# The final norm of a hybrid decoder: two of four token tiles finished by GpSimd and ScalarE instead of VectorE

## What is computed

```python
def rmsnorm(x, w):
    xf = x.astype(jnp.float32)
    y = xf * lax.rsqrt(jnp.mean(xf * xf, axis=-1, keepdims=True) + NORM_EPS)
    return (y * w.astype(jnp.float32)).astype(x.dtype)

def reference(x, ...):
    ...
        h = h + hier_moe(hn, router_group_w[l], router_group_b[l], router_expert_w[l],
                         router_expert_b[l], expert_w_gate[l], expert_w_up[l], expert_w_down[l])
    return rmsnorm(h, final_norm_w)
```

## Time and profile before

| | us |
|---|---|
| median of 3 runs | 2718.67 |
| the three runs | 2718.04, 2718.67, 2720.47 |
| the profiled execution's own time | 2721.2 |
| its span, first to last instruction | 2719.5 |
| experts' stage, read as one stretch | 1750 to 2680 |
| end of the program | 2680 to 2719.5 |

### The profile page before, as it was taken

How to read it: one execution, slowest core, us unless ns; L and a number is a source line. 1 busy time by engine, 2 the same in 40 slices (tenths; PEclk the granted TensorE clock), 3 DMA queues, 4 the chain that set the end, 5 groups by cost and what they waited for, 6 DMA issues and landing times.

```text
span 2719.5 us, 39968 instructions
## 1 busy us (share of the span) xinstructions
PE 2564.1 (94%) x15677; PEld 1715.6 (63%) x15677; DVE 1106.2 (41%) x1605; ACT 801.8 (29%) x986; POOL 103.9 (4%) x136
## 2 busy tenths in 40 slices
PE   7999999999999999999999999799988889888896
PEld 6888888887777777777788877343333333333342
DVE  5333333344556555556444322332323322333334
ACT  6333334433334443344222222111111111112112
POOL 0000000000000000000000000000000000000000
PEclk9999999999999999999999999799999999999998
DMA  5333333332322223223654532999999999999995
GB/s 167 103 98 108 108 105 95 101 101 73 96 69 64 79 79 89 59 80 86 217 152 142 176 109 110 387 421 421 422 422 422 422 421 422 422 421 422 422 421 214
DMA packets 312381, 594.38 MB, mean 219 GB/s; under 512 B 17098, under 2 KB 238918, under 8 KB 260550
## 3 DMA queue, kind: packets, MB, share of 16 engines
q1 hardware_dynamic: 303372, 559.71, 56.2%
q0 software_dynamic: 8912, 33.22, 3.2%
HBM read 578.02 MB, written 24.64 MB: 222 GB/s over the span
## 4 chain that ended last, share of the span: by engine, by line
PE 72%; DMA 18%; DVE 4%; issue 2%; ACT 2%; SPq 0%; DVEq 0%; ACTq 0%
PE in_z L160 34%; DMA ex_w_up<-in_expert_w_up_dram 17%; PE bank L2335 10%; PE bank L2362 4%; PE mg_z_rw L151 1%; PE mg_z_rw L150 1%; PE mg_z_rw L152 1%; PE in_z L151 1%; PE in_z L150 1%; PE in_z L152 1%; PE rw_b L1266 1%; PE rw_b L1257 1%; PE bank L2322 1%; DVE in_lo L192 1%; PE bank L2323 1%
## 5 line engine op out<-in xcount | busy, mean ns | idle before, releaser
L160 PE MATMUL in_z<-xn_hi,in_lo 128*128 128x512 f32 x1440 | 585.4, 407 | 0.0
L160 PE MATMUL in_z<-xn_hi,in_hi 128*128 128x512 f32 x1440 | 575.6, 400 | 5.9 <-DVE in_lo L192 4.4
L160 PE MATMUL in_z<-xn_lo,in_hi 128*128 128x512 f32 x1440 | 562.6, 391 | 0.0
L2335 PE MATMUL bank<-ex_w_gate,ex_xt_sb 128*64 128x512 f32 x768 | 356.6, 613 | 57.9 <-DMA ex_w_up<-in_expert_w_up_dram 57.9
L192 DVE TENSOR_TENSOR in_lo<-in_raw,in_hi 128x2048 fp32r<-128x2048 f32 x122 | 286.5, 2348 | 300.5 <-ACT in_hi L187 184.2
L2337 PE MATMUL bank<-ex_w_up,ex_xt_sb 128*64 128x512 f32 x768 | 357.5, 614 | 0.0
L160 PEld LDWEIGHTS in_z<-xn_hi,in_hi 128*128 128x128 f32 x1440 | 270.7, 188 | 70.1 <-issue 14.3
L160 PEld LDWEIGHTS in_z<-xn_hi,in_lo 128*128 128x128 f32 x1440 | 270.4, 188 | 62.5 <-issue 5.0
L160 PEld LDWEIGHTS in_z<-xn_lo,in_hi 128*128 128x128 f32 x1440 | 270.4, 188 | 61.4 <-issue 5.7
L2335 PEld LDWEIGHTS bank<-ex_w_gate,ex_xt_sb 128*64 128x64 f32 x768 | 104.1, 141 | 279.6 <-issue 279.6
L2362 PE MATMUL bank<-ex_w_down,const 128*64 128x512 f32 x512 | 228.8, 600 | 2.4 <-ACT const L2248 0.6
(11 more groups left out here) (487 smaller groups left out, 3417.6 us busy)
## 6 DMA issues: line engine op xcount, KB each, us to landing
ex_w_down<-in_expert_w_down_dram SPq DMA_DIRECT2D x128, 1024.0 KB, 21.2
ex_w_gate<-in_expert_w_gate_dram SPq DMA_DIRECT2D x96, 1024.0 KB, 21.4
ex_w_up<-in_expert_w_up_dram SPq DMA_DIRECT2D x96, 1024.0 KB, 25.5
in_raw<-in_w_in_dram SPq DMA_DIRECT2D x91, 1024.0 KB, 5.7
in_raw<-in_w_out_dram SPq DMA_DIRECT2D x32, 512.0 KB, 4.6
ex_w_gate0b<-in_expert_w_gate_dram SPq DMA_DIRECT2D x16, 1024.0 KB
ex_w_up0b<-in_expert_w_up_dram SPq DMA_DIRECT2D x16, 1024.0 KB
rt_then_ex_w<-in_expert_w_gate_dram SPq DMA_DIRECT2D x16, 1024.0 KB
```

Of the source, the lines that this page charges most:

```text
L160: return pe.matmul(out, w[:, k, :], x[:, k, :], start=(n == 0), stop=(n == PASSES * KT - 1), skip_group_check=True)
L2335: pe.matmul(gate_up[low, :], x_t[:, k, halves[u]], w_gate[n][u][:, j, :], start=start, stop=stop, skip_group_check=True)
```

## The change

GpSimd gets two operations at its end: tile 0 times `w_final` into a third dead weight tile, tile 1 times `w_final` into a fourth (`h_w`, both named after their first use, `ex_w_gate` and `ex_w_up`). It waits for the complete adds of the tile, not for the scale. ScalarE gets two operations behind its second root: it multiplies these two tiles by their scale, a per-partition factor, in place. They are stored from there. VectorE drops `finish(0)` and `finish(1)`, does all 16 adds in one run, then `scales(0)`, `scales(1)`, `finish(2)`, `finish(3)`. The stores are issued in the order tile 0, tile 2, tile 1, tile 3 in three pieces.

```diff
+    h_w = [w[1][0][:].rearrange("p j f -> p (j f)") for w in (w_gate, w_up)]
     LAST_BANKS = (6, 7, 2, 3, 4, 5, 0, 1)
-    pieces = [(t, slice(0, D)) for t in range(TT - 1)] + [
+    BY_ACT = 2
+    pieces = [(t, slice(0, D)) for t in range(BY_ACT, TT - 1)] + [
         (TT - 1, slice(0, D // 2)), (TT - 1, slice(D // 2, 3 * D // 4)), (TT - 1, slice(3 * D // 4, D))]
...
+    weighted, scaled = sems.sem("fin_weighted", "fin_scaled")
+    SCALE_STEPS = 6
...
-        for e in range(SPREAD - 2):
+        for e in range(SPREAD):
             last_add(e, base)
         scales(0)
-        finish(0)
-        for e in range(SPREAD - 2, SPREAD):
-            last_add(e, base)
-        finish(1)
         scales(1)
-        finish(2)
-        finish(3)
+        for t in range(BY_ACT, TT):
+            finish(t)
...
-        for n, (t, part) in enumerate(pieces):
-            sp.wait_ge(finished, n + 1)
-            sp.dma_start(io["out"][0, t * P:(t + 1) * P, part], h[:, t, part]).then_inc(stored, 16)
-        sp.wait_ge(stored, 16 * len(pieces))
+        def store(ready, n, src, t, part):
+            sp.wait_ge(ready, n)
+            sp.dma_start(io["out"][0, t * P:(t + 1) * P, part], src[:, part]).then_inc(stored, 16)
+
+        def store_piece(n):
+            t, part = pieces[n]
+            store(finished, n + 1, h[:, t, :], t, part)
+
+        store(scaled, 1, h_w[0], 0, slice(0, D))
+        store_piece(0)
+        store(scaled, 2, h_w[1], 1, slice(0, D))
+        for n in range(1, len(pieces)):
+            store_piece(n)
+        sp.wait_ge(stored, 16 * (len(pieces) + BY_ACT))
...
+        pool.wait_ge(w_final_in, 16)
+        for t in range(BY_ACT):
+            wait_apart(pool, keep["pool_waits"], added, 8 * n_blocks + 2 * TT + 2 * t + 2)
+            pool.tensor_tensor(h_w[t], h[:, t, :], w_final, ALU.mult).then_inc(weighted, 1)
...
+        act.wait_ge(dve_o, SCALE_STEPS)
+        for t in range(BY_ACT):
+            act.wait_ge(weighted, t + 1)
+            act.activation(h_w[t], h_w[t], ACT.Copy, scale=rstd[:, t:t + 1]).then_inc(scaled, 1)
```

## The result

| | before | changed |
|---|---|---|
| median of 17 runs, us | 2720.44 | 2726.80 |
| lowest to highest, us | 2718.04 to 2723.94 | 2722.74 to 2729.25 |
| profiled execution: its own time, us | 2721.2 | 2724.8 |
| its span, us | 2719.5 | 2722.8 |

The ratio of the changed kernel to the one before is 1.0022, with a 95% interval of 1.0014 to 1.0029: slower by 6.0 us, 3.8 to 7.9. The three runs known ahead of the prediction had a median of 2718.67; 17 runs of the same kernel have 2720.44.

What follows compares the result with a forecast made beforehand. The prediction took the final stores as the bound: first store at 2710.95 plus 13.8 gave a span end of 2724.7, 5.2 us later. Added to the median of 2718.67, that made 2723.9 us, range 2718.0 to 2726.0.

Steps and rivals of the forecast that it cites:

- second root: ScalarE's root after the second `var`, ahead of its scaling of tiles 0 and 1; forecast at 2708.9.
- first store to end: Output stores at the kernel's end: without pauses, the span ends 13.8 us after the first store is issued.
- The adds aren't held: VectorE's adds, one input in PSUM, stay 0.60 us apart beside GpSimd's products; the rival, adds held, had chance 0.08.
- Two-input operations are held until the running product ends: VectorE's `scales` chain: operations with two SBUF inputs wait for GpSimd's running product; `var` from 2699.95 to 2701.0.
- `ms` is held too: VectorE's one-input operation after `var` waits for GpSimd's second product, to 2705.7; argued from the speed of L298.
- the first rival: In VectorE's chain `ms` isn't held, but L2156 waits for 2705.7; span end 2722.7, time 2721.9 us; chance 0.27.
- Even undisturbed the change gains only 0.3 us: End of kernel without holds: first store 2.1 us later, removed pauses worth 2.4, span end 2719.2.
- The sum for the stores: Final output stores without pauses: first store + 0.7 + 10.2 of transfer + 2.9 to the end of the span.
- A product may be 3 us longer before that costs anything: GpSimd's products are done by 2705.7, ScalarE's first scaling starts at 2709.0, so 3 us longer was called free.
- I add differences of the span to the median: Whole-kernel time: the 5.2 us later span end added to the median before, 2718.67, giving 2723.9 us.
- The chance of slower: Whole-kernel verdict: slower 0.29, same 0.69, faster 0.02; 0.19 of the forecast's 0.45 went to slower.
- likeliest two cases: VectorE's chain at the end: `ms` held, 2723.9 us, chance 0.45; `ms` not held, 2721.9 us, chance 0.27.

Runs made afterwards that it cites:

- x1_tiny: Changed kernel with GpSimd's two products cut to 64 of 2048 columns; end +28.99 us from the first add, total 1.0004 of before.
- x2_half: Changed kernel with GpSimd's two products cut to 1024 of 2048 columns; end +30.28 us from the first add, against +34.39 in the changed kernel.
- x8_psum: Changed kernel with `var` kept in PSUM, so that `ms` reads it there; end +32.32 us from the first add, against +34.39 in the changed kernel.
- x4_memset: Changed kernel with GpSimd's two products replaced by six 128x2048 memsets; end +31.14 us from the first add, against +34.39 in the changed kernel.

## Why the prediction was right and where it was wrong

The mechanism and its size were right; the time on record, 2723.9 us with a range up to 2726.0, wasn't: 2726.80 was measured. By the steps of the prediction, in us from the first add:

| step | forecast | measured |
|---|---|---|
| GpSimd's product | 4.54 | 4.53, 4.49 |
| first product ends | +10.7 | +10.78 |
| `var` due, and held to | +9.7, +10.7 | +9.57, +10.80 |
| `ms` held to | +15.4 | +15.25 |
| second root | +18.6 | +18.32 |
| one scaling | 1.91 | 1.99 |
| first store | +20.7 | +20.44 |
| first store to end | 13.8 | 13.95 |
| difference of the end to before | 5.2 | 5.15 |

That the last row agrees to 0.05 us is in part luck: the first store came 0.25 us earlier than forecast, and the end followed it 0.15 us later.

- **The adds aren't held:** right, 0.60 us each with and without a product beside them.
- **Two-input operations are held until the running product ends:** right. x1_tiny and x2_half show that the loss comes and goes with it.
- **`ms` is held too:** right, though it was argued from a speed alone. x8_psum shows that it must read SBUF for that, and the time of the first rival came out when this condition was taken away. Reading SBUF isn't enough: the reciprocal does so with one input and isn't held (0.17 us). And it isn't only about reading, since a memset that reads nothing holds `ms` too (1.78 us). That `ms` uses both ways into SBUF fits all of these rows; no row shows the ways themselves.
- **Even undisturbed the change gains only 0.3 us:** right, 0.25. The sum for the stores holds in every kernel without a pause: 13.88 to 14.02 from first store to end in nine profiles of eight kernels.
- **"A product may be 3 us longer before that costs anything":** wrong, and against the working's own hold, by which `ms` waits for the second product's end. x2_half shows it from the other side: with products 2.2 us shorter each, the end comes 4.11 us earlier.
- **The base was wrong.** The working adds 5.2 us to 2718.67, the median of three runs. The kernel before has a median of 2720.44 in 17 runs, so this term was 1.8 us too low. Two of the three runs were among the lowest of a spread of 5.9 us. More runs leave the base unsure too: the three later sets of 15 runs of the same kernel, each on another chip, have medians of 2718.57, 2721.60 and 2720.41. The same sum on 2720.44 gives 2725.6, with 2726.8 measured. Of these last 1.2 us, 0.3 lie outside the span, a part that "differences of the span" leaves out; where they arise wasn't looked for. The rest is inside the interval of 3.8 to 7.9 us. The step that failed is "I add differences of the span to the median", with a range made of the cases at the end of the program and the price of the rates alone, and without a term for where the runs of before lie. That this matters is to be seen in the profiles: the first add starts anywhere between 2688.01 and 2691.41 in the eleven, while the 34.4 us behind it repeated within 0.05 us in the two profiles of the changed kernel, the only one profiled twice. The upper end of the range should have been 2 us or so higher.
- **The chance of slower was too low.** The forecast lay 0.2 us under the bound of 0.2%, and more than half of its weight was given to the side that it happened to lie on. I had also written that a measurement can't tell such a difference from no change. With 17 runs it can: the interval of 1.0014 to 1.0029 leaves no room for none. Whether the loss is above 0.2% isn't decided by it. A forecast of a loss of 0.19%, whose likeliest two cases were both losses of over 0.1%, should have been called a loss.

## What to carry to other kernels

Work handed to an idle GpSimd doesn't always run beside VectorE's work. Here each product of GpSimd that read SBUF held the VectorE operations with two inputs in SBUF, and the `tensor_scalar` with its input there, until it ended, however small they were; adds with one input in PSUM and a reciprocal ran on. The profile shows the held operation as busy. So look for chains of tiny operations under such work: 0.17 us became 4.42, and the chain was what everyone waited for. Where the end is made of stores, ask first what the first store and the pauses do: in x1_tiny VectorE finished 3.8 us earlier than before, and the end came 0.25 earlier. And before adding a small difference to a median, ask how far that median moves from one set of runs to the next; here it was up to 3 us.

## What the runs showed of the hardware

- A `tensor_scalar` from SBUF to SBUF is held by a GpSimd operation down to two or three columns (4.42 and 4.43 us). In x8_psum it isn't when it reads PSUM (0.16), nor is a reciprocal from SBUF (0.17); nor is an add of PSUM and SBUF (0.60 each). The Trainium skill ("SBUF — State Buffer", Who interferes with whom) gives this division by inputs and modes, and every row here agrees with it.
- In x4_memset a GpSimd memset holds that `tensor_scalar` (1.78 us), but not an operation with two inputs (0.16).
- Between two GpSimd products that follow each other without a gap in the profile (the first ends at 2699.19, the second starts at 2699.15), a VectorE operation that has waited gets in: `var` ended at 2699.21, and the second product wasn't longer for it (4.49).
- ScalarE's copy of 128x2048 in float32 with a scale per partition took 1.99 us, the one without 1.91 (median of 89, with a rounded output type, fp32r).
